# Seven-product pairs in runs of three and four in the up projection of a decoder layer

## The reference

```python
h2 = rmsnorm(x, g_ffn)                               # 520 x 1024
f = h2 @ w_up                                        # w_up: 1024 x 5632
f_gate, f_up = split(f, [2816])
f_conv, new_f = causal_depthwise_conv3(f_gate, buf_f, conv_f_w)
x = x + (silu(f_conv) * f_up) @ w_down               # w_down: 2816 x 1024
```

## Time and profile before

| | |
|---|---|
| median of three runs | 853.08 us |
| profiled execution | 853.01 us, its span 851.0 us |
| TensorE matmul busy | 839.0 us (99%), 6948 matmuls |
| TensorE weight loads busy | 834.9 us (98%) |
| VectorE busy | 665.1 us (78%) |
| ScalarE busy | 407.7 us (48%) |
| GpSimd busy | 128.9 us (15%) |
| weight loads of the up projection | 44 of 512 KB, 3.7 us to landing |

### The profile page before, as it was taken

One profiled execution on the slowest core, in us unless ns is written; L12 is line 12 of the kernel. 1 busy time (PEld: TensorE's weight loads), 2 busy tenths in 40 slices (PEclk: granted clock), 3 DMA queues, 4 the chain that ended last, 5 costly groups with the idle time before them and its releaser, 6 DMA issues.

```text
span 851.0 us, 18315 instructions
## 1 busy us (share of the span) xinstructions
PE 839.0 (99%) x6948; PEld 834.9 (98%) x6948; DVE 665.1 (78%) x983; ACT 407.7 (48%) x733; POOL 128.9 (15%) x98
## 2 busy tenths in 40 slices
PE   8999999999999999999999989999999999999996
PEld 7999999999999999999999989999999999999996
DVE  4899998999999966765579899988888888544343
ACT  7753646364342234663235665554454457232232
POOL 2283838475000000000002200000000000000000
PEclk9999999999999999999999999999999999999999
DMA  9423233432433332218732123333333334343323
GB/s 259 125 85 114 76 99 98 134 102 86 120 99 88 99 111 85 88 51 152 169 99 75 50 69 106 99 99 104 108 97 99 109 94 125 93 128 99 98 72 114
DMA packets 189160, 88.92 MB, mean 104 GB/s; under 512 B 34758, under 2 KB 187644, under 8 KB 189076
## 3 DMA queue, kind: packets, MB, share of 16 engines
q1 hardware_dynamic: 186225, 86.29, 36.3%
q10 hardware_dynamic: 2875, 1.82, 0.8%
HBM read 83.79 MB, written 3.51 MB: 103 GB/s over the span
## 4 chain that ended last, share of the span: by engine, by line
PE 94%; DVE 3%; ACT 1%; issue 1%; ACTq 0%; DVEq 0%
PE psum L1714 44%; PE psum L1720 22%; PE psum L1890 10%; PE psum L1918 6%; PE psum L1895 5%; PE psum L1923 3%; PE psum L2031 1%; PE psum L2040 1%; PE psum L1757 1%; PE psum L1764 0%; DVE w_lo L1363 0%; PE psum L1755 0%; PE psum L1692 0%; DVE u L1520 0%; ACT w_hi L815 0%
## 5 line engine op out<-in xcount | busy, mean ns | idle before, releaser
L1714 PE MATMUL psum<-act,w_hi 128*128 128x260 f32 x2600 | 341.1, 282 | 0.0
L1714 PEld LDWEIGHTS psum<-act,w_hi 128*128 128x128 f32 x2600 | 323.0, 188 | 0.0
L1068 DVE TENSOR_TENSOR w_lo<-raw,w_hi 128x1024 fp32r<-128x1024 f32 (+2 forms) x110 | 129.9, 1183 | 77.1 <-ACT w_hi L544 76.7
L1720 PE MATMUL psum<-act,w_lo 128*128 128x260 f32 x1300 | 185.1, 282 | 0.0
L1720 PEld LDWEIGHTS psum<-act,w_lo 128*128 128x128 f32 x1300 | 168.1, 188 | 0.0
L544 ACT ACTIVATE w_hi<-raw 128x1024 fp32r<-128x1024 f32 (+2 forms) x110 | 107.0, 976 | 88.2 <-PE psum L1720 85.7
L512 POOL TENSOR_TENSOR gate_a<-gate_a,prods 128x512 f32<-128x512 f32 x72 | 110.1, 1529 | 79.6 <-ACT prods L629 71.2
L1890 PE MATMUL psum<-act,w_hi 128*128 128x260 f32 x448 | 71.3, 283 | 2.8 <-ACT tmp L891 2.1
L1363 DVE TENSOR_TENSOR w_lo<-raw,w_hi 128x1024 fp32r<-128x1024 f32 x44 | 53.6, 1222 | 22.2 <-ACT w_hi L815 22.2
L1918 PE MATMUL psum<-mid,w_hi 128*128 128x260 f32 x512 | 68.0, 283 | 0.0
L1145 DVE SCALAR_TENSOR_TENSOR psum<-u,cst,psum 128x512 f32<-128x512 f32 x96 | 66.8, 747 | 0.0
(11 more groups left out here) (208 smaller groups left out, 997.8 us busy)
## 6 DMA issues: line engine op xcount, KB each, us to landing
raw<-in_w_in SPq DMA_DIRECT2D x56, 512.0 KB, 3.7
raw<-in_w_up SPq DMA_DIRECT2D x44, 512.0 KB, 3.7
raw<-in_w_down SPq DMA_DIRECT2D x16, 384.0 KB, 3.8
raw<-in_w_down SPq DMA_DIRECT2D x16, 320.0 KB, 3.1
v<-in_x_prompt SPq DMA_DIRECT2D x8, 512.0 KB, 6.3
raw<-in_w_b_out SPq DMA_DIRECT2D x8, 512.0 KB, 3.7
raw<-in_w_a_out SPq DMA_DIRECT2D x8, 512.0 KB, 5.4
raw<-in_w_o SPq DMA_DIRECT2D x8, 512.0 KB, 4.0
```

What stands on the lines that cost most here:

```text
L1068: ve.tensor_tensor(w_lo[:, slot, 0:k, :], raw[:, s, 0:k, :], w_hi[:, slot, 0:k, :], ALU.subtract).then_inc(lo_done, 1)
L1714: pe.matmul(a[:, h, :], w_hi[:, s, j, :], rhs(k, part)[:, h * H:(h + 1) * H], start=start and part == 0, stop=False)
L1720: last = pe.matmul(a[:, h, :], w_lo[:, s, j, :], rhs(k, 0)[:, h * H:(h + 1) * H], start=False, stop=stop)
```

## The change

The list of plain pairs becomes 0, 4, 8, 13, 17, 21. So 16 instead of 14 pairs have seven products, in runs of 3, 3, 4, 3 and 3. Pair 3, for example, was plain and now has seven products. A seven-product pair in the middle of a run follows another one and has another one behind it; the kernel before has none.

Bank X and the two gate banks are now given by a table that rotates over banks 0 to 3, and `banks_free` makes TensorE wait for whoever last used a bank, at P1 and at the gate of a plain pair. Ahead of the down projection there is a wait for the last up_product.

`weight_sums` is cut in two: `weight_sum_1` (one instruction) and `weight_sums_2` (two instructions). In a pair that follows a seven-product pair, weight_sums_2 and weight_sum_4 stand behind up_22; in one that doesn't, weight_sum_4 alone moves behind it.

```diff
-    PLAIN = tuple(range(0, FT, 3))
+    PLAIN = (0, 4, 8, 13, 17, 21)
...
-        gate_banks, up_banks = psum[:, 0:2, 0:H], psum[:, 4:6, 0:H]
+        up_banks = psum[:, 4:6, 0:H]
...
+        BANK_X = dict(zip((n for n in range(FT) if SEVEN[n]), (2, 3, 0, 3, 0, 1) + (2, 3, 0, 1) + 2 * (3, 0, 1)))
+        BANK_GATE = dict(zip(PLAIN, (0, 1, 2, 2, 2, 2)))
...
         def bank_x(n):
-            return psum[:, 2 if TURN[n] else 3, 0:H]
+            return psum[:, BANK_X[n], 0:H]
+
+        def gate_banks(n):
+            return psum[:, BANK_GATE[n]:BANK_GATE[n] + 2, 0:H]
+
+        def gate_in(n, bank):
+            return max((m for m in PLAIN if m < n and bank in (BANK_GATE[m], BANK_GATE[m] + 1)), default=None)
+
+        def chain_in(n, bank):
+            return max((m for m in range(n) if BANK_X.get(m) == bank), default=None)
...
-            def weight_sums(n):
+            def weight_sum_1(n):
...
                 ve.tensor_tensor(s1_s2[:, 0], raw_even(up), raw_odd(up), ALU.add).then_inc(w_sum, 1)
+
+            def weight_sums_2(n):
+
+                gate, up = raw_at(n, "gate"), raw_at(n, "up")
                 ve.wait_ge(w_sum, 4 * NTH[n] + 1)
                 ve.tensor_tensor(s1_s2[:, 1], s1_s2[:, 0], raw_even(gate), ALU.subtract).then_inc(w_sum, 1)
                 ve.tensor_tensor(raw_even(up), raw_even(gate), raw_even(up), ALU.subtract).then_inc(w_sum, 1)
...
                 lo_open(n + 1)
                 if SEVEN[n + 1]:
-                    weight_sums(n + 1)
+                    weight_sum_1(n + 1)
+                if not FOLLOWS[n] and SEVEN[n + 1]:
+                    weight_sums_2(n + 1)
                 if FOLLOWS[n]:
                     up_product(n - 1)
                 else:
                     plain_product(n - 1)
+                up_22(n)
+                if FOLLOWS[n] and SEVEN[n + 1]:
+                    weight_sums_2(n + 1)
                 if SEVEN[n + 1]:
                     weight_sum_4(n + 1)
-                up_22(n)
...
+            def banks_free(n, bank):
+
+                if chain_in(n, bank) is not None:
+                    pe.wait_ge(prod_done, START + 2 * KT + chain_in(n, bank) + 1)
+                if gate_in(n, bank) is not None:
+                    pe.wait_ge(cx_set, gate_in(n, bank) + 1)
...
-                    pe.wait_ge(cx_set, PLAIN[PLAIN.index(n) - 1] + 1)
-                    plain(n, "gate", gate_banks, 1, at_4=lambda: fourth(n - 1))
+                    for bank in (BANK_GATE[n], BANK_GATE[n] + 1):
+                        banks_free(n, bank)
+                    plain(n, "gate", gate_banks(n), 1, at_4=lambda: fourth(n - 1))
...
-                if last_x(n) is not None:
-                    pe.wait_ge(prod_done, START + 2 * KT + last_x(n) + 1)
+                banks_free(n, BANK_X[n])
                 product("P1", n)
...
             pe.wait_ge(cx_set, FT)
+            pe.wait_ge(prod_done, START + 2 * KT + FT - 1)
             down(0, 0)
```

More of the change, by code:

```diff
@@ L310, in build @@
         assert PLAIN[0] == 0 and PLAIN[-1] == FT - 1 and SEVEN[1]
+        BANK_X = dict(zip((n for n in range(FT) if SEVEN[n]), (2, 3, 0, 3, 0, 1) + (2, 3, 0, 1) + 2 * (3, 0, 1)))
+        BANK_GATE = dict(zip(PLAIN, (0, 1, 2, 2, 2, 2)))
+        assert len(BANK_X) + len(BANK_GATE) == FT
         def bank_x(n):
-            return psum[:, 2 if TURN[n] else 3, 0:H]
+            return psum[:, BANK_X[n], 0:H]
[5 more added lines that the diff above has]
+            return max((m for m in range(n) if BANK_X.get(m) == bank), default=None)
         def banks_zy(n):
             return psum[:, 4:6, 0:H] if TURN[n] else psum[:, 6:8, 0:H]
-        def last_x(n):
-            return max((m for m in range(n) if SEVEN[m] and TURN[m] == TURN[n]), default=None)
         def last_zy(n):
@@ L1456, in plain_gate @@
                     conv_in_free(n)
-                ve.tensor_tensor(halves(cx[:, PADB:PADB + N]), gate_banks, halves(rinv), ALU.mult).then_inc(cx_set, 1)
+                ve.tensor_tensor(halves(cx[:, PADB:PADB + N]), gate_banks(n), halves(rinv), ALU.mult).then_inc(cx_set, 1)
             def plain_product(n):
@@ L1949, in plain_pair @@
                     pe.wait_ge(evicted, out_of(G_O + KT - 2))
-                    plain(n, "gate", gate_banks, 1)
+                    plain(n, "gate", gate_banks(n), 1)
                 else:
-                    pe.wait_ge(cx_set, PLAIN[PLAIN.index(n) - 1] + 1)
-                    plain(n, "gate", gate_banks, 1, at_4=lambda: fourth(n - 1))
+                    for bank in (BANK_GATE[n], BANK_GATE[n] + 1):
+                        banks_free(n, bank)
+                    plain(n, "gate", gate_banks(n), 1, at_4=lambda: fourth(n - 1))
                     pe.wait_ge(c1_set, NTH[n])
```

## The result

The changed kernel takes 860.26 us (median of 4 runs, 860.12 to 860.38), against 853.05 us (4 runs) beside it: ratio 1.0084, 95% interval 1.0067 to 1.0101. It is slower by 7.2 us. Forecast were 858.4 us and a range up to 860.2: the sign and the mechanism came as forecast, the size did not, by 1.9 us, and the time lies just outside the range.

What follows compares the result with a forecast made beforehand. The prediction took TensorE, 99% busy, as the bound, with VectorE setting the pace in middle pairs. Span 851.0 - 2.88 (matmuls) + 8.23 (stalls) = 856.4, plus 2.0 around it: 858.4 us; 8-in-10 range 855.0 to 860.2.

Steps and rivals of the forecast that it cites:

- The removed matmuls: TensorE, up projection: two pairs change from plain to seven products, 24 matmuls fewer, 2.88 us less work.
- The middle pair's length: VectorE's step in a pair between two seven-product pairs: 11.90 us, where TensorE needs 10.08 us.
- the point from which P7 stalls: A pair's P7 stalls when lo_2 starts over 1.45 us after P1, by the excess plus 0.11 us.
- waits of 0.8 to 2.3 us for up_v: Sign of being right: TensorE idle that long for ScalarE's copy in pairs 3, 7, 11, 12, 16 and 20.
- TensorE stays the bound: Rival: late VectorE loses its 1.34 us idle, middle step 10.56 us, only pair 3 stalls; 851.2 us, chance 0.08.
- the 850.1 us: Time by the skill's rule to relieve the engine of highest occupancy: TensorE's whole 2.88 us would be saved.
- A wait on VectorE's own result costs 0.21 us at up_22: up_22 starts 0.55 us after up_product's second half, not 0.34; without this, step 11.69 us, time 856.5 us, chance 0.16.
- The runs 14 to 16 and 18 to 20, and pairs 11 and 12: New stalls: 0.89 us in each of the two runs; 0.89 us in pair 11 and 1.82 us in pair 12.
- Pairs 5 to 7: Run of seven-product pairs: pair 6 does not stall, pair 7 stalls 1.32 us.
- the window from pair 3 to the down projection: Sign of being right: this part of the up projection, 203.4 us before, grows by 5.4 us.
- Edits I cost at nothing: Bank waits of P1(9), P1(14), P1(18) for plain_gate, tie at P4, weight loads, wait before down projection: 0 us.
- more is lost: Rival: P1 waits for plain_gate three times at 0.7 us, plus 0.11 us in five stalled pairs; 861 us, chance 0.04.

Runs made afterwards that it cites:

- dve_order: The changed kernel with turn_root as in root_end and VectorE's order up_gate, lo_2, lo_4, conv_rest, lo_3 in pairs following a seven-product pair: 850.34 us.
- act_order: The changed kernel with turn_root as in root_end, VectorE's order unchanged, and hi_3 ahead of conv_first on ScalarE in pairs following a seven-product pair: 851.31 us.
- five_plain: dve_order with plain pairs 0, 5, 11, 16, 21, so 17 seven-product pairs, and banks reassigned to match: 849.91 us.
- root_end: The changed kernel with turn_root taken out of the pairs and put behind the last up_lo: 858.61 us.
- chain9_bank1: The changed kernel with the chain of pair 9 in bank 1 instead of 2, turn_root left in step 8: 859.38 us.
- root_4: The changed kernel with turn_root in the step of plain pair 4 instead of 8: 860.02 us.

## Why the prediction was wrong, and where it was right

- *The removed matmuls, 2.88 us.* Right: 24 fewer, and dve_order stands 2.6 us under the kernel before, with 0.96 us lost in pair 3 and 0.62 gained in pair 2 (2.88 - 0.96 + 0.62 = 2.54).
- *The middle pair's length, 11.90 us, and the point from which P7 stalls.* Right to the hundredth (11.90 twice; P7(3) at 522.97 for 522.98). dve_order and act_order show that the reason was right too: the 1.34 us are a loop over ScalarE, and both ways of cutting it take away all new stalls but 0.9 to 1.0 us in pair 3 and, in act_order, 0.4 in pair 12. One sign that I named was off: waits of 0.8 to 2.3 us for up_v. The trace has 0.23 or 0.24 us there, and the rest of each stall two products earlier, at P6 for up_1; since both copies hang on the same chain, the sum is that of P7 all the same. The rival "TensorE stays the bound" failed on this. So did the 850.1 us that followed from the rule of the Trainium skill, "Perfetto Trace Analysis", section "Identifying the Most-Contended Engine": the weight loads filled 98% of the span, TensorE was relieved, and the time rose by 7.2 us; only where the chain over VectorE and ScalarE had become shorter too (dve_order, act_order, five_plain) did the relief arrive.
- *A wait on VectorE's own result costs 0.21 us at up_22.* In the middle step up_22 at 514.46 follows the second half of up_product at 513.91 by 0.55 us, as before. The Trainium skill, page "VectorE: DVE Perf Modes", section "The DRAIN you can't avoid", says of a row of copies that the semaphore costs nothing extra. Carried over to this wait, it would have made the step 11.69 us; it was 11.90.
- *The runs 14 to 16 and 18 to 20, and pairs 11 and 12.* Right within 0.03 us each.
- *Pairs 5 to 7: 1.32, measured 1.51.* A start was misread: I took P1(5) from the chain of waits (535.28) and all other starts from the timeline, which has it at 535.12. So lo_2(5) was 1.00 us behind P1(5), not 0.84, and lo_2(6) is now 1.03 behind P1(6) (548.61 and 547.58). The same offset is in 716.84, which the timeline has at 716.67: the window from pair 3 to the down projection grew by 7.1 us, for 5.4 forecast.

```profile
535.12 0.87 PE L1890 MATMUL psum<-mid,w_hi 128*128 128x260 f32 x6
```

- *The failed step: "Edits I cost at nothing", the wait of P1(9), P1(14) and P1(18) for plain_gate, "I take 0, since the cover is in the same pair".* It holds for 14 and 18. For 9 the cover was gone, by an instruction sequence that no line of the diff touches: turn_root is tied to the third entry of the list that the diff changes. In the trace before it ran in step 6, where P1(7) had no such wait and pair 8 had slack. I did not follow the list's name to its other uses. The term "0" was 1.59 us, and the forecast's miss is this and pair 7's 0.19 us (sum of stalls 10.04 against 8.23). root_end, which takes that one term out, measures 858.61 us for the forecast 858.4. Taken apart by chain9_bank1 and root_4, about half of the price is the bank's wait; the other half is VectorE's lag, which the pairs behind pay wherever turn_root stood ahead of a run of three or four (pairs 4 and 8).
- *The range.* The case "more is lost", 861 us, had the right place, P1 behind plain_gate, but 0.04 of the chance, because it was priced as three small waits and not as one that something could push.

What stays open is why the clock fell behind pair 1's wait in some executions (last section); it cost no time here.

## What to carry to other kernels

Where two engines hand work to each other several times in one step, the step's length is that of the chain through both, not the busier engine's sum: lay it out from start to start in the trace, add the idle time that the chain contains, and compare it with the step of the engine that should be the bound. Lag in such a schedule is a stock that any pair can spend and only slack gives back, so small work is placed where nothing waits behind it. And when a constant of the schedule changes, look for everything that is indexed by it.

## What the runs showed of the hardware that I had not expected

The repeatability: from lo_2 to lo_2 the two-engine chain came out the same within 0.02 us in pairs of different kernels (11.88 to 11.90, in five pairs of the changed kernel and in root_4 and chain9_bank1), so that a schedule laid out by hand from rows of one trace held over 200 us. TensorE after a wait shows the same 0.10 to 0.11 us more in its first six matmuls (0.98 or 0.99 for 0.88 us; 0.96 at P1(9)) for waits from 0.15 to 1.9 us.

The granted clock is not the same in every execution. In all ten profiled executions TensorE waits 1.9 us ahead of P7(1), until about 498.8. In five of them (before, after, root_4, chain9_bank1, dve_order) the clock stays at 1.00; in the other five it is 0.50, the lower level of 1.2 GHz, from about 500 to 503 us, although the changed kernel and root_end, for example, have the same instructions up to there. Six matmuls then take 1.50 us for 0.88. The view by windows (the third value from the end is the granted clock) in dve_order and in five_plain, and TensorE's row of five_plain:

```profile
500.50:503.00 2.50, 2.50 (x23) 2.50 (x22) 2.47 (x5) 0.00 (x0) 0.00 (x0) 1.00 0.76 210
...
500.50:503.00 2.50, 2.50 (x13) 2.50 (x13) 2.46 (x4) 0.00 (x0) 0.00 (x0) 0.50 0.69 205
...
500.71 1.50 PE L1910 MATMUL psum<-mid,w_hi 128*128 128x260 f32 x6
```

It cost no time, because TensorE would have waited in pair 2 or 3 anyway: from P1(1) to P1(3) root_end takes 22.98 us and the changed kernel 22.97. But where a wait of pair 2 or 3 is missing from one of these traces, this can be the reason, and not the edit.
